# Expert weights of a two-layer hybrid backbone in quarters, with more of them in dead buffers; value tiles in token rows; fewer warm-up products

## The reference, cut to what matters

```python
def ab_stream(h, w_in, b_in, ...):
    q, k, v, r, glr, z, xs, bm, cm, dt = split_cols(h @ w_in + b_in, AB_SPLITS)   # v: 1024 columns

def expert_choice_ffn(h, router_w, w1, w3, w2):
    aff = jax.nn.softmax((h @ router_w).astype(F32), axis=-1)
    gates, idx = lax.top_k(jnp.swapaxes(aff, 1, 2), cap)
    xe = jnp.take_along_axis(h, idx[..., None], axis=1).reshape(bsz, N_EXPERTS, cap, d)
    hid = jax.nn.silu(jnp.einsum('becd,edf->becf', xe, w1)) * jnp.einsum('becd,edf->becf', xe, w3)
    ye = jnp.einsum('becf,efd->becd', hid, w2) * gates[..., None].astype(h.dtype)
    return jnp.zeros_like(h).at[jnp.arange(bsz)[:, None], idx].add(ye.reshape(bsz, N_EXPERTS * cap, d))

# layer 0: the MoE over latent and context tokens (two streams); layer 1: over the latent tokens alone
```

## Time and profile before

| | |
|---|---|
| median of 3 runs | 2248.63 us (2245.6 to 2249.2) |
| profiled execution | 2246.18 us |
| its span, first to last instruction | 2244.5 us |
| mean granted TensorE clock | 0.957 |
| PE / PE weight loads / DVE / ACT / POOL busy | 86% / 46% / 32% / 22% / 7% |
| DMA moved | 527 MB, mean 235 GB/s |

### The profile page before, as it was taken

One profiled execution on the slowest core, in us unless ns is written; L12 is line 12 of the kernel. 1 busy time (PEld: TensorE's weight loads), 2 busy tenths in 40 slices (PEclk: granted clock), 3 DMA queues, 4 the chain that ended last, 5 costly groups with the idle time before them and its releaser, 6 DMA issues.

```text
span 2244.5 us, 31117 instructions
## 1 busy us (share of the span) xinstructions
PE 1939.5 (86%) x13454; PEld 1022.4 (46%) x13454; DVE 712.0 (32%) x1320; ACT 499.0 (22%) x1066; POOL 162.4 (7%) x208
## 2 busy tenths in 40 slices
PE   6999889999999998888989999989999965666566
PEld 3444644445445333333336566677887721212112
DVE  1121743254304001010116877566674300000001
ACT  2332421234003000000013323444442200000001
POOL 0000000020000000000004000044450000000000
PEclk9999999999999999999999999999999987878878
DMA  9111221150118999999993543300002599999996
GB/s 384 53 65 65 96 115 75 75 225 1 37 75 338 428 430 429 431 431 430 428 423 134 207 163 115 123 2 2 2 2 113 225 420 429 431 432 432 430 431 270
DMA packets 34937, 527.44 MB, mean 235 GB/s; under 512 B 2416, under 2 KB 3696, under 8 KB 18544
## 3 DMA queue, kind: packets, MB, share of 16 engines
q1 hardware_dynamic: 33184, 522.55, 55.4%
q10 hardware_dynamic: 1616, 2.89, 0.4%
HBM read 524.39 MB, written 1.05 MB: 234 GB/s over the span
## 4 chain that ended last, share of the span: by engine, by line
PE 49%; DMA 30%; DVE 9%; issue 5%; PEld 3%; ACT 2%; DVEq 1%; PEldq 0%; ACTq 0%; SPq 0%; POOL 0%
DMA ring<-in_moe_w 29%; PE bank L564 15%; PE bank L1152 11%; PE bank L1044 5%; PEld bank L564 3%; PE bank L1003 3%; DVE ring L2031 2%; DVE x L1869 2%; PE bank L789 2%; PE bank L766 2%; DMA ring<-in_mod_w 1%; DVE x L2431 1%; PE bank L714 1%; PE bank L472 1%; PE bank L670 1%
## 5 line engine op out<-in xcount | busy, mean ns | idle before, releaser
L564 PE MATMUL bank<-hT,ring 128*128 128x512 f32 (+1 forms) x1504 | 547.3, 521 | 3.7 <-ACT hT L1319 1.4
L1152 PE MATMUL bank<-ring,xgs 128*32 128x512 f32 x3048 | 389.6, 666 | 136.5 <-DMA ring<-in_moe_w 135.1
L564 PEld LDWEIGHTS bank<-hT,ring 128*128 128x128 f32 x1504 | 281.1, 190 | 249.1 <-issue 227.6
L1152 PEld LDWEIGHTS bank<-ring,xgs 128*32 128x32 f32 x3048 | 108.5, 120 | 391.1 <-issue 300.7
L1152 PE MATMUL bank<-ring,hT 128*32 128x512 f32 x1488 | 198.8, 690 | 77.9 <-DMA ring<-in_moe_w 77.9
L2277 DVE SCALAR_TENSOR_TENSOR x<-bank,modT,x 128x256 f32<-128x256 f32 x96 | 42.2, 480 | 466.5 <-PE bank L1178 466.5
L1152 PEld LDWEIGHTS bank<-ring,hT 128*32 128x32 f32 x1488 | 56.5, 124 | 207.3 <-issue 164.1
L1869 DVE SCALAR_TENSOR_TENSOR x<-gluR,cols,x 128x256 f32<-128x256 f32 x240 | 116.0, 484 | 16.3 <-issue 0.6
L2266 DVE TENSOR_TENSOR hT<-mrow,bank 128x512 f32<-128x512 f32 x16 | 10.9, 683 | 184.8 <-PE bank L1152 184.8
L2266 DVE TENSOR_TENSOR hT<-small,bank 128x512 f32<-128x512 f32 x8 | 5.5, 687 | 178.4 <-PE bank L1152 178.4
L1585 ACT ACTIVATE xgs<-bank 128x512 f32<-128x512 f32 x24 | 14.3, 597 | 205.4 <-PE bank L1124 205.4
(11 more groups left out here) (493 smaller groups left out, 2345.9 us busy)
## 6 DMA issues: line engine op xcount, KB each, us to landing
ring<-in_moe_w SPq DMA_DIRECT2D x93, 4096.0 KB, 22.1
ring<-in_mod_w SPq DMA_DIRECT2D x12, 4096.0 KB, 13.8
ring<-in_cd_w SPq DMA_DIRECT2D x6, 4096.0 KB, 14.3
ring<-in_ab_w SPq DMA_DIRECT2D x4, 4096.0 KB, 20.8
ring<-in_ab_wo SPq DMA_DIRECT2D x2, 4096.0 KB, 14.5
ring<-in_cd_wo SPq DMA_DIRECT2D x2, 4096.0 KB, 13.8
early<-in_moe_w SPq DMA_DIRECT2D x2, 2048.0 KB, 24.0
ring<-in_moe_w SPq DMA_DIRECT2D x2, 2048.0 KB, 18.6
```

The costliest lines, as they stand in the source:

```text
L564: last = mm(ps[p["no"] % 4][:, p["c0"]:T], w[:, k, :], hT[:, k, p["c0"]:T], start=(k == 0), stop=(k == KD - 1))
L1152: last = mm(ps[banks + s][32 * j:32 * j + 32, :], lhs[s][:, 4 * kh + k, 32 * j:32 * j + 32], piece(g, n, 4 * k + j), start=(kh == 0 and k ...
```

## The change

It has four parts.

1. `v` is made in token rows: the tokens stand still, four value tiles move at once, and the result needs no transpose. A row of biases comes by one more DMA (`gla_bv`) and POOL adds it. The eight value tiles become one group, so the tile `k3` comes after them.
2. The ring becomes a circle of 12 quarters (1.05 MB each). From group 3 on an expert load is one quarter (groups 3 to 8) or two, and may be issued as soon as the quarter 12 places earlier is used (`quarter_used`), not the whole group. Landing is counted on four semaphores `stream`.
3. More pieces lie outside the ring: in layer 0 `early` is loaded at the SSD's end and half of group 3 goes to `hT` once the tokens are turned; in layer 1 all of group 3 and three quarters of group 4 go to ten places, each as soon as it is dead.
4. `keep_warm` ahead of the first gather has 3 products for 10 in layer 0, and 2 for 6 in layer 1.

Some semaphores share a name now (`kv`, `head_mixed`, `norm_squared`), and POOL clears `act_c` for DVE.

```diff
-AB_GLA = [("small", 0)] + [("q", i) for i in range(4)] + [("k", i) for i in range(4)] \
-    + [("v", i) for i in range(8)] + [("r", i) for i in range(8)]
+AB_GLA = [("small", 0)] + [("q", i) for i in range(4)] + [("k", i) for i in range(3)] \
+    + [("v", i) for i in range(8)] + [("k", 3)] + [("r", i) for i in range(8)]
...
+SPARE = {0: [(RING, 0), (RING, 1)], 1: [(RING, q) for q in range(4)] + [(RING + 1, q) for q in range(3)]}
+EARLY = [(12 * Q - 1, 0), (12 * Q - 1, 1)]
+def ring_place(layer, gi, q):
+    return 4 * MOE_SLOT[layer] + 4 * gi + q - sum(s < (gi, q) for s in SPARE[layer] + EARLY)
+def expert_loads(layer, gi):
+    if gi < RING:
+        return [(0, 4)]
+    if gi == 12 * Q - 1:
+        return [(3, 1)]
+    quarters = [q for q in range(4) if (gi, q) not in SPARE[layer]]
+    step = 1 if gi < 3 * RING else 2
+    loads = []
+    for i in range(0, len(quarters), step):
+        q, n = quarters[i], min(step, len(quarters) - i)
+        if n == 2 and ring_place(layer, gi, q + 1) % (4 * RING) == 0:
+            loads += [(q, 1), (q + 1, 1)]
+        else:
+            loads.append((q, n))
+    return loads
...
+            def free(gi, q):
+                g, k = order[order.index((gi, q)) - 4 * RING]
+                if k == 3:
+                    sp.wait_ge(w_used, first + g + 1)
+                else:
+                    sp.wait_ge(sg("quarter_used"), 36 * Q * layer + 3 * g + k + 1)
+            if layer == 0:
+                sp.wait_ge(sg("ssd_y"), 8)
+                sp.dma_start(early[:, :], part(last, 0, 4096)).then_inc(early_in, 16)
+                for gi in range(RING):
+                    whole(gi)
+                sp.wait_ge(sg("htok_turned"), 2 * NT)
+                sp.dma_start(hT[:, :, :].rearrange("p k t -> p (k t)"), part(RING, 0, 4096)).then_inc(spare_in, 16)
+            else:
+                sp.wait_ge(sg("gdn_O"), KD)
+                whole(0)
...
+                sp.wait_ge(sg("head_turned"), GH + 4)
+                sp.dma_start(hT[:, :, 0:SEQ], part(RING, 0, 2048).rearrange("p (k t) -> p k t", t=SEQ)).then_inc(spare_in, 16)
+                sp.dma_start(early[:, :], part(last, 0, 4096)).then_inc(early_in, 16)
+                whole(1)
+                whole(2)
+                sp.wait_ge(sg("x_ready"), 3)
...
+                sp.wait_ge(sg("htok_turned"), 3 * NT)
...
+                sp.wait_ge(sg("logits_turned"), 2)
...
+            for gi in range(RING, 12 * Q):
+                if gi == last:
+                    free(gi, 2)
+                    sp.dma_start(ring_quarters(layer, gi, 2), part(gi, 4096, 2048)).then_inc(early_in, 16)
+                for q, n in expert_loads(layer, gi):
+                    free(gi, q + n - 1)
+                    sp.dma_start(ring_quarters(layer, gi, q, n), part(gi, 2048 * q, 2048 * n)).then_inc(stream[gi % 4], 16)
...
+                        if p["how"] == "token":
+                            t, e0 = p["i"] % NT, 4 * (p["i"] // NT)
+                            for k in range(KD):
+                                last = mm(ps[p["no"] % 4].rearrange("p (e c) -> p e c", c=P), hT[:, k, t * P:t * P + P], w[:, e0:e0 + 4, k, :],
+                                          start=(k == 0), stop=(k == KD - 1))
...
                     for k in range(4):
...
+                        if expert_loads(layer, g) and k == expert_loads(layer, g)[0][0]:
+                            if g < RING:
+                                pe.wait_ge(landed[n % RING], rg.landed[n])
+                            else:
+                                pe.wait_ge(stream[g % 4], stream_landed(layer, g))
...
+                        if k < 3:
+                            last.then_inc(sg("quarter_used"), 1)
                     last.then_inc(w_used, 1)
...
-                keep_warm(6 if layer else 10, 5)
+                keep_warm(2 if layer else 3, 5)
...
+            def gla_values():
+                pool.wait_ge(consts_in, 80)
+                for p in PLAN["gla"]:
+                    if p["how"] == "token":
+                        pool.wait_ge(sg("proj_evacuated"), p["no"] + 1)
...
+                        G.tensor_tensor(v, v, vbias[:, e, :], ALU.add).then_inc(sg("v_biased"), 1)
```

More of the change, by code:

```diff
@@ L50, with stream_landed @@
 CONF_STEPS = [(0, 7), (7, 13), (13, 19), (19, 25), (25, 31)]
+RING = 3
 CD_HALVES = {9: (1, 0), 18: (1, 1), 28: (2, 0), 32: (2, 1)}
+SPARE = {0: [(RING, 0), (RING, 1)], 1: [(RING, q) for q in range(4)] + [(RING + 1, q) for q in range(3)]}
+MOE_SLOT = (2, 2)
+EARLY = [(12 * Q - 1, 0), (12 * Q - 1, 1)]
[16 more added lines that the diff above has]
+    return loads
+def stream_landed(layer, gi):
+    return 16 * sum(len(expert_loads(m, g)) for m in range(layer + 1) for g in range(RING, 12 * Q)
+                    if g % 4 == gi % 4 and (m < layer or g <= gi))
 def weight_groups():
@@ L68, in weight_groups @@
     g += mod(1, 0)
-    g += [("moe0", i, 1) for i in range(12 * Q)]
+    g += [("moe0", i, int(i < RING)) for i in range(12 * Q)]
     halves = mod(1, 1) + mod(1, 2)
@@ L89, in __init__ @@
         self.groups = weight_groups()
-        self.first, self.at, self.landed = {}, {}, []
+        self.first, self.at, self.landed, self.place = {}, {}, [], []
         total = [0] * RING
@@ L96, in __init__ @@
             self.landed.append(total[n % RING])
+            self.place.append(n - (n >= self.first.get("moe0", n) + 12 * Q) * (len(SPARE[0]) + len(EARLY)) // 4)
 def hybrid_backbone(nc, A, out):
     rg = Ring()
+    assert tuple(rg.place[rg.first[f"moe{layer}"]] % RING for layer in range(2)) == MOE_SLOT
     with ExitStack() as ctx:
@@ L248, in spaces @@
                 return got
-            lent = ring[:, rg.first["moe1"] % RING, :, :].rearrange("p j n -> p (j n)")
+            lent = ring[:, rg.place[rg.first["moe1"]] % RING, :, :].rearrange("p j n -> p (j n)")
             glf = gluR[:, :, :, :].rearrange("p a b c -> p (a b c)")
@@ L269, in hybrid_backbone @@
         spare_in = sem("spare_in")
+        stream = [sem(f"stream{i}") for i in range(4)]
         consts_in = sem("consts_in")
@@ new lines, in load_experts, with part, whole @@
+            order = [(gi, q) for gi in range(12 * Q) for q in range(4) if (gi, q) not in SPARE[layer] + EARLY]
+            def part(gi, c0, n):
+                return A["moe_w"][layer, gi, :, c0:c0 + n]
+            def whole(gi):
+                sp.wait_ge(w_used, first + gi - RING + 1)
+                sp.dma_start(slot(first + gi).rearrange("p j n -> p (j n)"), part(gi, 0, 8192)).then_inc(landed[(first + gi) % RING], 16)
+            def free(gi, q):
[4 more added lines that the diff above has]
+                    sp.wait_ge(sg("quarter_used"), 36 * Q * layer + 3 * g + k + 1)
@@ L559, in project @@
                             pe.wait_ge(sg("proj_evacuated"), p["no"] - 3)
[L560 to L561 removed]
+                        w = slot(p["group"]).rearrange("p a (b k c) -> p (a b) k c", b=2, k=KD)
+                        if p["how"] == "token":
[3 more added lines that the diff above has]
+                                          start=(k == 0), stop=(k == KD - 1))
+                        for k in range(0 if p["how"] == "token" else KD):
                             if j == 0 and ready is not None:
                                 h_wait(pe, ready, k)
[L564 removed]
+                            last = mm(ps[p["no"] % 4][:, p["c0"]:T], w[:, p["place"], k, :], hT[:, k, p["c0"]:T],
                                       start=(k == 0), stop=(k == KD - 1))
@@ L2499, in _ @@
             G = nc.gpsimd
+            G.memset(act_c[:, :, :], 0.0)
             G.memset(ident[:, :], 0.0)
```

138 lines of the change are left out of this document (72 added, 66 removed).

## The result

The changed kernel takes 2228.36 us (median of 4 runs, 2225.54 to 2228.87), the kernel before 2248.39 beside it: a ratio of 0.9911 (95% interval 0.9893 to 0.9928), 20.0 us less. The prediction said 2218 with a range of 2208 to 2230. So direction and range held, but a third of the expected gain did not come. Its sum was made against the profiled execution: 2246.18 to 2217.4. The profiled execution after took 2228.23 (span 2226.5): 18.0 us were gained where the sum has 28.8, and 10.8 are to be found. The measured 2228.4 also lies outside the forecast's own 2212 to 2226, in the stretch that the prediction gave to the rival "the spares fill less" (2226 to 2236), and what follows shows that this rival did not come about. That the range held is in part luck.

A forecast was written before the change was run, and what follows sets the result against it. Both expert stages were taken to last as long as their bytes do; 3.3 + 4.9 + 4.9 + 3.4 + 19.1 + 1.2 - 8 = 28.8 us took 2246.18 to 2217.4, stated as 2218, range 2208 to 2230 (8 in 10).

The forecast's parts named there:

- the spares fill less: Rival: holes at the start of both expert stages stay, up to 8.4 and 4.9 us; 2231 (2226 to 2236), chance 0.11.
- Part 1: Value tiles before the GLA: the transposes of eight tiles leave PE's chain, 0.41 us each, 3.3 us gained.
- Part 2, layer 0's stream: Layer 0's expert loads: holes filled, 6.9 us down to 2.0, gain 4.9; two quarters fewer in the queue, gain 4.9.
- small pieces: Expert streams of both layers: shorter rows cost 1% of the rate, 4 us a layer, -8 us; bounds 0 and 24.
- The tail of layer 0: End of layer 0's expert stage: last product 5.7 us behind the last byte where it was 9.1, gain 3.4 us.
- Between the stages: Layer 1's projections start as much earlier as layer 0's tail ends; no further gain or loss counted.
- Layer 1, 19.1 + 1.2 - 4: Layer 1's expert stage: stream ends 19.1 us earlier, tail gains 1.2, shorter rows cost 4.
- Part 4: Fewer warm products before the gathers: starts 1.0 us earlier in layer 0, 0.6 in layer 1, inside the other terms.
- the slow pieces: Rival: both expert streams run at 409 GB/s, the smallest pieces' rate, each piece having its own completion; 2255, chance 0.05.
- keep its rate: Rival: longer queues of small loads still run at 430 GB/s, so 8 us come back; 2210 (2206 to 2212), chance 0.20.

The follow-up runs named there:

- four spares: The changed kernel with layer 1's spare pieces cut from seven quarters to four, group 4's coming with the stream; 2234.43 us.
- The corrected kernels: The changed kernel with a separate wait for group 46's second half: 2223.70 us; the same with larger loads from group 9 on: 2218.24 us.

## Why the prediction was right, and where it was not

What bounds the kernel was read rightly, and so was every mechanism of the sum but one: the expert streams set both stages, and bytes moved earlier, filled holes and the price of short rows made the result. By the terms of the sum:

- *Part 1, 3.3 us.* 3.7 stood at the GLA's first transposes, and 1.65 arrived at the first expert load, because the clock fell once behind a gap that I took as given. In the three executions without a drop 3.1 to 4.1 arrive. Right in kind and size, less one drop of 1.6.
- *Part 2, layer 0's stream, 4.9 + 4.9, less 4 for small pieces: 5.8.* Group 46 starts 4.94 us earlier, counted from the first load (473.62 for 478.56). The holes gave their term: 7.2 - 2.3 = 4.9 by the windows. So 9.8 - 4.94 = 4.9 us are left for the price, for my 4. By the windows' rates, over the stream's 44 groups (38.5 in halves at 427 GB/s, 5.5 in quarters at 421; the section on the change has 44.5), it is some 4; by the distances of the landings it would be 38.5 x 0.129 + 5.5 x 0.264 = 6.4, but these contain the groups that landed late.
- *The tail of layer 0, 3.4 us: the step that failed.* "After, the second half of 46 lands 4.9 us before the last byte; PE does it". PE does not: its wait counts all loads of a group, and so two whole groups stand behind 46's landing as before (13.93 us for 13.94). It gained nothing. The corrected kernels show that the size was nearly right: 3.0 where the clock holds, as PE is the bound from 45's landing on, and 1.3 where it falls in group 45.
- *Between the stages, nothing expected.* 536.00 for 534.24. In eleven executions it is 534.58 to 534.75; in the two (the change, and four spares) where the GDN's 32 products at 1482 ran 1.98 and 1.97 us for 1.15 it is 536.0 and 536.1. So 1.4 of these 1.8 us are a clock drop.
- *Layer 1, 19.1 + 1.2 - 4 = 16.3 us.* 13.1 came. Group 46 lands 12.3 us earlier behind the first load (505.35 for 517.63) where the stream's terms have 15.1. The price was 38.5 x 0.099 + 4.25 x 0.226 = 4.8 for 4. The stream stood at its full rate by 1784, which is 1788.8 in the time of before, where I had 1788: 0.8 late. 1.2 are left without a place, which is what two executions of this stage differ by. Behind 46's landing the tail takes 8.72 us for 9.56: 0.8 for 1.2, as the group is again done whole.
- *Part 4.* Product 0 of layer 0 came 1.1 us earlier behind the first load, as said. With the warm products back the stage took as long, so this was worth nothing that can be seen; in layer 1 it may be worth 0.4.

The missing 10.8 by stage are 1.65 + 0.85 + 3.4 + 1.75 + 3.2 (10.85, by rounding); by cause, 3.8 from the two tails, 3.05 from two clock drops, 1.65 from the price in both layers, 0.8 from the start of layer 1, and 1.55 without a place. That split of the small terms rests on one profile of each kernel. Of the rivals, the slow pieces had a right part, that rows set the rate, at a fifth of the way: 427 GB/s, not 409. What the rival argued with, that each piece ends with its own completion, is not it: the number of loads cost nothing. The stream did not keep its rate, and the spares filled what they should.

The Trainium skill, "DMA: Bandwidth & Descriptors", section "Anatomy of one DMA — SWDGE (gpsimd) path", has a fixed cost of about 2 us for each DMA on GpSimd's path. In these queues, fed from SP, no fixed cost shows: 1.33 and 4 loads for each group take 9.980 and 9.983 us. Nor did the 341 GB/s show that the prediction weighed for pieces of 1 MB: single quarters ran at 421.

## What to carry to other kernels

Where a queue is never empty, ask how long the rows of a load are, not how many loads there are: cut a load finely only where the finer release fills a hole, and where the queue is full keep the rows long. Before a gain is counted from a piece that lands earlier, look at what the waiting engine counts, and then at whether that engine has the time: a piece that lands early is worth nothing behind a wait for the whole group, and less than it seems behind an engine that is still at the group ahead. And read a change's first stages in more than one profile: one clock drop was as large here as half of part 1.

## What the runs showed of the hardware

- A load's rate in a full queue follows its rows: 431 GB/s with 32 KB for each partition, 427 mostly with 16, 421 with 8, 409 with 4; in layer 1 9.3 ns more for each row on a DMA engine, from 8 to 64 rows for a group (9.757 to 10.273 us). The number of loads, and gaps of 24 KB between rows of 8 KB, cost nothing that can be seen.
- Behind the same gap of 2.8 us, with the same products ahead of it, TensorE's clock held 2.4 GHz in 5 executions and fell towards 1.2 in 7 (14 products took 1.94 us, or 2.44 to 3.57), at 1.6 us each. Behind a gap of 1.71 us it fell in two executions, one with the gap ahead filled and one without. The same drop of 0.8 us in 32 products cost 1.4 us in one place and nothing one step earlier, where PE had to wait anyway.
